# First expert step fed by seven of nine row tiles; the sample rows pass the output projection ahead of the last prompt tile

## What is computed

```python
x <- LN1(alpha*x + (sig(g_a)*(A @ w_branch_a) + sig(g_b)*(B @ w_branch_b)) @ w_out)
x <- LN2(alpha*x + MoE(x))
...
aff = sigmoid(xt @ w_router)                     # 16 experts in 4 groups of 4
grp = (aff + b_router).reshape(n_tok, 4, 4)
g_sel = argmax(sum(top_k(grp, 2)[0], -1), -1)    # the best group, in it the best two experts
wts = aff[eid] / sum(aff[eid])
out = ragged_dot(silu(ragged_dot(xs, w_gate, sizes)) * ragged_dot(xs, w_up, sizes), w_down, sizes)
```

## Time and profile before

| | |
|---|---|
| median of 3 runs | 1908.28 us (1908.01 to 1908.91) |
| span of the profiled execution | 1907.2 us |
| outside the span (median minus span) | 1.1 us |
| PE busy over the span | 97% |
| DVE, ACT, POOL busy over the span | 61%, 48%, 25% |
| products of `w_out` | 1291 to 1408 us |
| from the last of them to `gate(1)` | 1408 to 1456.4 us |
| steps 1 to 23 on PE | 1456.4 to 1872 us |

### The profile page before, as it was taken

How to read it: one execution, slowest core, us unless ns; L and a number is a source line. 1 busy time by engine, 2 the same in 40 slices (tenths; PEclk the granted TensorE clock), 3 DMA queues, 4 the chain that set the end, 5 groups by cost and what they waited for, 6 DMA issues and landing times.

```text
span 1907.2 us, 31779 instructions
## 1 busy us (share of the span) xinstructions
PE 1856.5 (97%) x11644; PEld 1663.7 (87%) x11645; DVE 1164.8 (61%) x1628; ACT 917.4 (48%) x1536; POOL 481.8 (25%) x643
## 2 busy tenths in 40 slices
PE   8999999999999999999999999999989999999997
PEld 8999988899999988889888898998857888888884
DVE  5544355642212359998999989644467587644756
ACT  3243330211210358888888888311123576645755
POOL 0000000000000215555555554002111244322333
PEclk9999999999999979999999999999988999999998
DMA  5234252232313410000000000524254798877865
GB/s 173 82 109 120 78 173 56 67 113 89 113 52 86 133 31 1 1 2 1 2 2 1 2 2 12 173 72 174 83 211 159 276 393 293 293 280 238 317 225 189
DMA packets 113735, 232.60 MB, mean 122 GB/s; under 512 B 25034, under 2 KB 81906, under 8 KB 107442
## 3 DMA queue, kind: packets, MB, share of 16 engines
q1 hardware_dynamic: 106162, 205.81, 30.5%
q0 software_dynamic: 7456, 25.17, 5.2%
HBM read 190.33 MB, written 42.71 MB: 122 GB/s over the span
## 4 chain that ended last, share of the span: by engine, by line
PE 53%; DVE 4%; ACT 3%; issue 1%; POOL 1%; DMA 0%; ACTq 0%; POOLq 0%; DVEq 0%
PE ps L3020 20%; PE ps L2069 6%; PE ps L2048 5%; PE ps L2690 5%; PE ps L254 4%; PE ps L2023 3%; PE ps L2025 3%; PE ps L3008 1%; DVE small L2133 1%; PE ps L2015 1%; PE ps L3069 1%; ACT turned_high L2238 1%; PE ps L2074 1%; PE ps L2676 1%; ACT region_w L2227 1%
## 5 line engine op out<-in xcount | busy, mean ns | idle before, releaser
L2133 DVE TENSOR_REDUCE small<-ps 128x1 f32<-128x640 f32 (+7 forms) x256 | 179.8, 703 | 26.3 <-PE ps L2015 24.4
L2157 DVE TENSOR_TENSOR turned_low<-ps,turned_high 128x512 fp32r<-128x512 f32 (+2 forms) x304 | 176.6, 614 | 12.0 <-ACT turned_high L2238 8.4
L2312 POOL TENSOR_SCALAR region_w<-region_w,small,gates 128x640 f32<-128x640 f32 (+7 forms) x172 | 141.7, 834 | 131.5 <-DVE small L2137 131.5
L2238 ACT CAST turned_high<-ps 128x512 fp32r<-128x512 f32 (+2 forms) x304 | 155.0, 531 | 31.6 <-PE ps L2048 28.2
L2023 PE MATMUL ps<-key_stacks,query_stacks 128*128 128x256 f32 (+3 forms) x384 | 142.0, 370 | 15.9 <-ACT region_w L2227 8.7
L2069 PE MATMUL ps<-turned_high,value_stacks 128*128 128x256 f32 (+1 forms) x608 | 152.1, 286 | 0.0
L2069 PE MATMUL ps<-turned_low,value_stacks 128*128 128x256 f32 (+1 forms) x608 | 142.2, 279 | 0.0
L2227 ACT ACTIVATE region_w<-ps,small 128x640 f32<-128x640 f32 (+7 forms) x172 | 121.7, 708 | 24.8 <-DVE small L2133 20.1
L3020 PE MATMUL ps<-gate_parts,rows_parts 128*128 128x512 f32 x552 | 131.7, 394 | 0.0
L3020 PE MATMUL ps<-down_parts,hidden_parts 128*128 128x512 f32 x552 | 131.1, 393 | 0.0
L3020 PE MATMUL ps<-up_parts,rows_parts 128*128 128x512 f32 x552 | 128.9, 389 | 0.0
(11 more groups left out here) (507 smaller groups left out, 4978.0 us busy)
## 6 DMA issues: line engine op xcount, KB each, us to landing
region_k<-in_w_gate SPq DMA_DIRECT2D x16, 2048.0 KB, 9.6
region_k<-in_w_up SPq DMA_DIRECT2D x16, 2048.0 KB, 10.1
region_w<-in_w_down SPq DMA_DIRECT2D x16, 2048.0 KB, 12.7
region_w<-in_w_in SPq DMA_DIRECT2D x16, 512.0 KB, 4.3
small<-gate_a SPq DMA_DIRECT2D x8, 516.0 KB, 3.4
region_w<-gate_b SPq DMA_DIRECT2D x8, 516.0 KB, 3.8
region_k<-in_x_prompt SPq DMA_DIRECT2D x8, 512.0 KB, 8.1
region_k<-in_w_in SPq DMA_DIRECT2D x8, 512.0 KB, 4.4
```

Of the source, the lines that this page charges most:

```text
L2133: nc.vector.tensor_reduce(nmax[:, n % 4:n % 4 + 1], sc, AX.X, ALU.max, negate=True).then_inc(s_max, 1)
L2157: nc.vector.tensor_tensor(lo, m.ps[:, turn_bank(G), 0:w], hi, ALU.subtract).then_inc(s_lo, 1)
L2238: nc.scalar.copy(hi, m.ps[:, turn_bank(G), 0:w]).then_inc(s_hi, 1)
L2312: nc.gpsimd.tensor_scalar(probs(H, t), probs(H, t), rec[:, H % 4, t:t + 1], m.gates[:, 2 * p + t, col:col + 1], ALU.mult, ALU.mult).then_i ...
```

## The change

What is moved and replaced:

- Tile order of the output stage: `OUT_ORDER` = 0 to 6, then the 8 sample rows (tile 8), then tile 7. `EARLY` = 7.
- The first step's rows are found from the first seven tiles alone: `choose(0, 7)`, `count_first`, `place_first`, `find_first` now stand inside the output stage, and POOL gathers them from the first seven tiles' rows in DRAM (`gather_first`).
- The turns and router products of the sample rows and tile 7 are moved behind the last `w_out` product and alternate with the passes of step 0: turn step 0's rows, turn samples, gate pass 0, route samples, turn tile 7, gate pass 1, route tile 7, up pass 0. The count for all rows follows, then gate pass 2 and the other up passes.
- Three of the four half low parts of expert 0's gate and up weights are made by POOL (`low_half`) and no more by DVE. ACT takes the up halves one at a time between the tiles' work (`split_half`).
- `place_pairs` has four more small steps, which keep step 0 for early rows alone (`hole`, `late`); with 157 early rows for expert 0, `hole` is 0 and the number of steps stays 24.
- `keep_awake`: 12 + 12 before step 0 and 8 before `gate(1)` go; 6 ahead of the count, 16 ahead of `find_rows` and 4 behind it come. The order of turning step 1's rows and step 0's hidden rows is swapped.

The core of the diff:

```diff
-NSTEP = NE + (NPAIR - 1) // P
+NSTEP = NE + (NPAIR + P - 1) // P + 1
+OUT_ORDER = (*range(TT - 1), TT, TT - 1)
+EARLY = TT - 1
...
     @block.gpsimd
+        def gather_first():
+            pool.wait_ge(rs.s_x1_out[0], 16 * 2 * EARLY)
+            pool.wait_ge(rs.s_erow, 1)
+            nc.gpsimd.indirect_dma_start(
+                out=m.RW[:, 4096:4096 + DM], out_offset=None, in_=m.x1_dram[0:EARLY * P, :],
+                in_offset=bass.IndirectOffsetOnAxis(ap=m.row_first[:], axis=0)).then_inc(rs.s_xfirst, 16)
...
     @block.tensor
+                if i == EARLY and k == 2:
+                    ro.route(pe, i - 2)
+                if i == EARLY and k == 4:
+                    ro.turn(pe, i - 1)
+                if i == EARLY and k == 7:
+                    ro.route(pe, i - 1)
+                if i == TT and k == 4:
+                    count_first()
+                if i == TT and k == 6:
+                    find_first()
...
     @block.vector
+        choose(nc, dve, m, rs, 0, EARLY)
+        place_first()
+        residual(EARLY)
+        moments(EARLY)
+        keep_first()
+        centred(EARLY)
+        keep_hole()
+        residual(TT)
+        moments(TT)
+        scaled(EARLY)
+        centred(TT)
+        scaled(TT)
...
     @block.gpsimd
+        def low_half(q, i):
+            part = slice(i * HALF, (i + 1) * HALF)
+            pool.wait_ge(s_hi[q], i + 1)
+            nc.gpsimd.tensor_tensor(wparts[q][:, 1, part], raw_third(m, q)[:, part], wparts[q][:, 0, part],
+                                    ALU.subtract).then_inc(s_lo[q], 1)
...
-        pool.wait_ge(m.sem_x1, 16 * 2 * NT9)
-        pool.wait_ge(s_row0, 1)
-        nc.gpsimd.indirect_dma_start(
...
+        low_half(GATE, 1)
+        pool.wait_ge(ro.s_x1, NT9)
+        low_half(UP, 0)
+        pool.wait_ge(ro.s_r, NT9)
+        low_half(UP, 1)
...
     @block.tensor
-        keep_awake(12)
-        count()
-        find_first()
-        keep_awake(12)
-        turn_rows(0)
-        first_products(m.ps[:, 0, :], wg, GATE).then_inc(s_g, 1)
-        first_products(m.ps[:, 1, :], wu, UP).then_inc(s_u, 1)
-        find_weights()
-        turn_rows(1)
-        turn_hidden(0)
-        keep_awake(8)
+        pe.wait_ge(ro.s_z, TT)
+        turn_rows(0)
+        ro.turn(pe, EARLY)
+        pe.wait_ge(ro.s_z, NT9)
+        first_pass(GATE, 0)
+        ro.route(pe, EARLY)
+        ro.turn(pe, TT)
+        first_pass(GATE, 1)
+        ro.route(pe, TT)
+        first_pass(UP, 0)
+        keep_awake(6)
+        count()
+        first_pass(GATE, 2).then_inc(s_g, 1)
+        first_pass(UP, 1)
+        first_pass(UP, 2).then_inc(s_u, 1)
+        keep_awake(16)
+        find_rows()
+        keep_awake(4, 6)
+        find_weights()
+        turn_hidden(0)
+        turn_rows(1)
...
     @block.scalar
+        act.wait_ge(ro.s_mm, NT9)
         high(GATE, 0)
-        high(UP, 0)
         rows_high(0)
+        ro.keep_turned(act, EARLY)
+        split_half(UP, 0)
+        ro.affinity(act, EARLY)
+        ro.keep_turned(act, TT)
+        split_half(UP, 1)
+        ro.affinity(act, TT)
...
     @block.vector
-        place_first()
+        rows_low(0)
+        low_halves(GATE, 0, (0,))
+        dve.wait_ge(ro.s_aff, NT9)
+        choose(nc, dve, m, rs, EARLY, NT9)
         place_pairs()
         place_lanes()
-        rows_low(0)
-        low(GATE, 0)
         keep_rows()
-        low(UP, 0)
```

More of the change, by code:

```diff
@@ L2485, in __init__ @@
         self.mx, self.mm = take(NT9), take(NT9)
+        self.early_upto, self.early_rank, self.early_end, self.hole = take(EARLY), take(EARLY), take(1), take(1)
+        self.early_lanes = m.nc.alloc_sbuf_tensor_at("early_lanes", [P, EARLY * P], BF16, offset=m.at_RW + 4 * 5120)[:].rearrange(
+            "p (t x) -> p t x", x=P)
+        self.s_ecnt, self.s_elanes, self.s_efound, self.s_erow, self.s_estep = (
+            m.sem("r_early_" + n) for n in ("counted", "lanes", "found", "row", "steps"))
         self.s_bias, self.s_clear, self.s_consts, self.s_choice = (
             m.sem("r_" + n) for n in ("bias", "clear", "consts", "choice"))
-        self.s_turned, self.s_chosen = m.sem("o_turned"), m.sem("r_chosen")
+        self.s_x1_out = [m.sem_x1, m.sem("x1_last_out")]
+        self.s_chosen, self.s_xfirst = m.sem("r_chosen"), m.sem("e_rows_in")
         self.choices = 0
@@ L2658, in _, with count_first, find_first @@
     @block.tensor
     def _(pe):
-        def turn(t):
+        def count_first():
+            pe.wait_ge(rs.s_chosen, 1)
+            nc.tensor.matmul(counted[:, 0:EARLY], rs.ones_b, rs.chosen_b[:, 0:EARLY], start=True, stop=True, skip_group_check=True)
+            nc.tensor.matmul(counted[:, EARLY:2 * EARLY], rs.place_b, rs.chosen_b[:, 0:EARLY], start=True, stop=True,
+                             skip_group_check=True).then_inc(rs.s_ecnt, 1)
+        def find_first():
+            pe.wait_ge(rs.s_elanes, 1)
+            for t in range(EARLY):
+                last = nc.tensor.matmul(found, rs.early_lanes[:, t, :], rs.token_b[:, t, :],
+                                        start=(t == 0), stop=(t == EARLY - 1), skip_group_check=True)
+            last.then_inc(rs.s_efound, 1)
@@ L2727, in settle, with residual, moments @@
+        def residual(i):
+            t, b = OUT_ORDER[i], i % 2
+            n = rows_of(t)
+            dve.wait_ge(s_mm, i + 1)
+            if i + 2 < NT9:
+                low_y(i + 2)
+            dve.wait_ge(s_x[i % 3], 16 * (i // 3 + 1))
+            src = m.ps[0:n, 2 * b:2 * b + 2, :].rearrange("p a c -> p (a c)")
+            stt(out=x1[t], in0=x1[t], scalar=ALPHA, in1=src, op0=ALU.mult, op1=ALU.add).then_inc(s_z, 1)
+        def moments(i):
+            t = OUT_ORDER[i]
             n, x = rows_of(t), x1[t]
-            stt = nc.vector.scalar_tensor_tensor
+            stats, mv = ro.stats[i == TT], ro.mv[i == TT]
+            dve.wait_ge(s_z, i + 1)
@@ L2756, in _, with centred, scaled @@
-        dve.wait_ge(s_aff, NT9)
-        choose(nc, dve, m, rs, TT - 1, NT9)
+        def centred(i):
+            t = OUT_ORDER[i]
+            n, x = rows_of(t), x1[t]
+            dve.wait_ge(s_mv, i + 1)
+            stt(out=x, in0=x, scalar=ro.mv[i == TT][0:n, 0:1], in1=gain[0:n], op0=ALU.subtract, op1=ALU.mult).then_inc(s_norm, 1)
+        def scaled(i):
+            t = OUT_ORDER[i]
+            n, x = rows_of(t), x1[t]
+            dve.wait_ge(s_norm, i + 1)
+            dve.wait_ge(s_rstd, i + 1)
+            stt(out=x, in0=x, scalar=ro.rstd[i == TT][0:n], in1=bias[0:n], op0=ALU.mult, op1=ALU.add).then_inc(s_x1, 1)
@@ new lines, in _ @@
+        dve.wait_ge(s_c, 48)
+        for i in range(EARLY):
+            residual(i)
+            moments(i)
+            centred(i)
+            scaled(i)
+        dve.wait_ge(rs.s_bias, 16)
+        dve.wait_ge(rs.s_consts, 1)
+        dve.wait_ge(s_aff, EARLY)
+        choose(nc, dve, m, rs, 0, EARLY)
[8 more added lines that the diff above has]
+        scaled(EARLY)
@@ L2786, in route_experts_and_combine @@
     upto, pos = take(NQ), take(NQ)
-    rank0, upto0 = (take(NT9) for _ in range(2))
-    nt, T, Tex = (take(NE) for _ in range(3))
+    nt, T, Tex, cnt = (take(NE) for _ in range(4))
+    late = take(NT9)
     more = take(NE * NKX)
@@ L2827, in route_experts_and_combine @@
     s_v, s_cnt, s_pairs, s_found = (m.sem("r_" + n) for n in ("step", "counted", "pairs", "rows_found"))
-    s_lanes0, s_found0, s_row0 = (m.sem("r_first_" + n) for n in ("lanes", "found", "row"))
     s_rows, s_pw, s_wfound, s_wlow, s_weights, s_table = (m.sem("r_" + n) for n in (
@@ L2832, in route_experts_and_combine @@
     s_hi, s_lo = ([m.sem(f"e_{n}_{w}") for w in ("gate", "up", "down")] for n in ("high", "low"))
[L2833 removed]
+    s_x, s_t, s_xh, s_xl = rs.s_xfirst, *(m.sem("e_rows_" + n) for n in ("turned", "high", "low"))
     s_g, s_u, s_silu, s_h, s_ht, s_hh, s_hl = (m.sem("e_" + n) for n in (
@@ L3270, in place_pairs @@
             step(tt(pos, pos, m.ps[:, 7, 0:NQ], ALU.add))
+            step(ts(late, pos[:, 0:NT9], rs.early_end, rs.hole, ALU.is_ge, ALU.mult))
+            step(tt(pos[:, 0:NT9], pos[:, 0:NT9], late, ALU.add))
             for c in range(2):
```

304 lines of the change are left out of this document (152 added, 152 removed).

## The result

The changed kernel takes **1916.92 us** in the median of 4 runs (1914.69 to 1919.85); the kernel before, on the same chip, 1908.60 (4 runs, 1908.01 to 1910.76). The ratio is 1.0040, 95% interval 1.0026 to 1.0054: **slower**, by 5 to 10 us. The profiled execution of the changed kernel took 1914.69 us with a span of 1912.9.

A forecast was written before the change was run, and what follows sets the result against it. PE bounds the kernel, so any shift of `gate(1)` shifts the end. The collision and low clock add 5.0 to 6.6 us, mean 5.8: span 1907.2 to 1913.0, plus 1.1 for the median: 1914.1 us, range 1905.5 to 1917.

The forecast's parts named there:

- tile 7 ready: Output stage: tile 7's residual and scaling done at 1416.5 us, 6.2 us plus one more 1.28 us operation for the samples.
- last router product: Behind the output stage: ends at 1423 to 1427 us, taken as 1425.5, against 1415.9 before.
- count of all rows: Behind the last `choose`: at 1435.2 us with POOL's halves colliding, 1430.0 without.
- The collision: POOL's half low parts hold DVE up around `choose`; count at 1435.2 in place of 1430.0. Forecast 57%, no collision 30%.
- reading part of 4.2 us: The part of POOL's 4.5 us subtraction, after its start-up, during which DVE would have to wait.
- The order in which the halves hit: DVE's last scaling, then POOL's gate half to 1420.7, DVE's gate half to 1422.9, POOL's up halves to 1427.1 and 1431.8.
- POOL's queue: Said to set the count, which hardly depends on the last router product; through at 1431.8, then 3.4 us to the count.
- near zero: The change without collisions: the stretch up to `gate(1)` ends between 1.0 us earlier and 0.6 later.
- The clock term: `gate(1)` runs at the low clock behind PE's waits for weights and split, losing 1.5 to 3.1 us.
- Nothing in the loop: From step 1 to the loop's end PE is always busy at full clock; nothing there can gain or lose.
- forecast span of 1913.0: Span of the profiled execution: 1907.2 before plus 5.8, the mean of +5.0 to +6.6.
- the forecast's own 1911.5 to 1916.5: Range of the median for the collision case alone, around 1914.1 us, chance 57%.

The follow-up runs named there:

- e1: The changed kernel with no half low part on POOL, DVE making them, and 8 more fillers ahead of `find_rows`; ratio to the kernel before 1.0008.
- e2: The changed kernel with each of POOL's three subtractions 256 columns wide in place of 2048, same waits, DVE writing zeros; ratio to the kernel before 1.0026.
- e5: The changed kernel with each half low part on POOL cut into 8 subtractions of 256 columns; ratio to the kernel before 1.0035.
- e10: e6 with only the last up half given back to POOL, released by the last router product; ratio to the kernel before 1.0019.
- b1: The kernel before with one 128x2048 subtraction added on POOL, released by the same sigmoid as the last `choose`; ratio to the kernel before 1.0012.
- e9: e6 with only the second gate half given back to POOL; ratio to the kernel before 0.9999.
- e6: e1 with more filler in PE's waits behind the count; ratio to the kernel before 0.9996.
- b2: The kernel before with 10 fillers ahead of `find_weights` and 12 in place of 8 ahead of `gate(1)`; ratio to the kernel before 1.0003.
- e3: The changed kernel with 15 fillers in place of 4 ahead of `find_weights` and 9 more ahead of `gate(1)`; ratio to the kernel before 1.0008.
- e8: e6 where SP waits for step 1's gathered rows before loading expert 1's up weights; ratio to the kernel before 0.9995.
- e11: e8 with 18 fillers on PE in its wait for step 0's rows; ratio to the kernel before 0.9985, 1907.44 us against 1910.14.

## Why the prediction was right

In us behind the last `w_out` product (the prediction's times less 1408.5):

| step | predicted | measured |
|---|---|---|
| rows of step 0 landed | 4.8 | 4.1 |
| tile 7 ready | 8.0 | 11.6 |
| last router product | 17.0 (14.5 to 18.5) | 16.6 |
| count of all rows | 26.7 | 26.9 |
| rows found | 39.6 | 39.6 |
| `gate(1)` starts | 51.5 | 53.0 |
| end of `gate(1)` against before | +5.0 to +6.6 | +6.1 |

- **The collision** is shown by e1, e2, e5, e10 and b1. Its share of the count is 5.2 us in the prediction, 5.2 in e2 and 6.0 in e1; without it the prediction had the count at 21.5 and e2 at 21.7. The rule of the Trainium skill's *SBUF — State Buffer*, Who interferes with whom (two SBUF inputs on DVE against a GpSimd instruction that reads SBUF, whoever issues first keeps the shared port for its whole instruction), is what these runs show up to 4.5 us, and the reduction in e5 keeps to it from the other side. The step from a wait of 0.30 us in the earlier trace rows to 4.5 held. (The prediction's reading part of 4.2 us is 4.3 by its own 2.1 ns a column; nothing hangs on it.)
- **The order in which the halves hit** was wrong, and that the count still came out, 26.9 for 26.7, is partly luck. I let DVE's last scaling go ahead of POOL's gate half; POOL was 0.08 us earlier. That made tile 7 late by 4.3 us and DVE's own half late, so that POOL's last half itself waited 1.5 us and fell on the first operation of `choose`. POOL's queue did not set the count alone, as the prediction said: POOL began 2.0 us earlier than predicted but then idled twice, 1.16 us for tile 7 and 0.43 for the router product. It was through at 22.7, not 23.3, and then all of `choose` but its first operation was still to come, 4.1 us with the counting and not 3.4. The two errors cancel. e9 shows that the early wait cost little.
- **Router products 8 to 9 us later are no loss of their own.** e6 has the changed order and is 0.55 us shorter than b2 at the same clock; the prediction's "near zero" without collisions (-1.0 to +0.6) is right at equal clock. As a forecast of what the kernel does without filler it is too low: e1 has no collision and is 2.4 us longer than before. It also has one half of 2.2 us on DVE behind the lanes; how much is that and how much the clock is not shown.
- **The clock term was too small.** I had 1.5 to 3.1 us, and only for `gate(1)`. For `gate(1)` alone that is right at its low end (1.5 against before). But e3 gives back 4.0: `gate(1)` 7.16 us for 5.54, but also `find_weights` 4.05 for 2.20 and the turned rows 1.91 for 1.06. `find_weights` went into the sum with the 2.78 of the earlier trace rows, where the clock fell halfway through; now, with a wait of 3.47 us ahead of it, it ran at the low clock from its start and was 1.3 us longer. This is most of the 1.5 us by which `gate(1)` started late. The two errors cancel in the end of `gate(1)`: it starts 1.5 us later than predicted and itself loses the least that I had allowed.
- **Nothing in the loop** waits more than before: 445.1 us from `up(1)` on in both.
- **The median** is 2.8 us above the 1914.1 forecast, though the profiled span, 1912.9, is 0.1 from the forecast span of 1913.0. It lies 0.4 us above the forecast's own 1911.5 to 1916.5 and 0.1 below the end of the whole range, 1917: that it is inside is luck. The profiled execution was the fastest of four. In the profiles what differs between executions lies ahead of the `w_out` products' end and goes with the clock around 700 us; whether this made the other three longer is not shown, since they have no profile.

What stays open: why the low clock around 700 us lasts longer in some executions than in others with the same code, why the timed runs of b2, e5 and e8 don't follow the ruler, and how short e11 would be with its fillers counted to its own waits.

## What to carry to other kernels

A wide two-input operation on GpSimd is not free work beside VectorE: it stops each two-input VectorE operation for its whole length, and hurts most when its release is the same event that starts a chain of small ones. Look for it not in idle time but in operations that take several times their usual length. When work moves ahead of a serial chain, the matrix engine's queue empties behind it: price what follows at the low clock, and count fillers so that they end before the wait they cover, because at the low clock they take longer (six took 2.67 us for 1.47 in e9) and become the wait.

## What the runs showed of the hardware

- A POOL subtraction of 128x2048 f32 takes 4.53 to 4.59 us, 2.2 ns a column, in the 7 cases of these traces that did not wait (the changed kernel, e3, b1, e9, e10); the estimate from 256 and 512 columns was 4.5.
- A wait for the port is booked as busy time of the waiting instruction on either engine (DVE 0.19 to 4.48 us, POOL 4.55 to 6.08).
- An extra delay can cost less than its length: of b1's 4.2 us at the count 3.4 reached the start of `find_weights` and 1.9 the end of `gate(1)`; the last 1.5 went because the clock behind was 1.00 (over 1450.5 to 1463.0), where before had 0.50 over 1449.5 to 1456.0.
- A gather of 128 rows issued 1.2 us behind a 2 MB load landed after 7.9 us (e6); without the load after 4.3 (e8) and 4.4 (e11).
- The granted clock over 680 to 740 us was 0.77 in six executions and 0.74 in eight, and the latter ended the `w_out` products 1.6 to 4.0 us later than the former.
